# Gated linear recurrence in a hybrid decoder layer: key factor moved into the exponent as a logarithm, four-deep buffer ring

## What is computed

```python
q = silu(q); f = lb + (1 - lb) * sigmoid(f_logit)
k = 1 - f
b = cumsum(log(f))                       # inside a chunk of tokens
att[t, s] = sum_c q[t,c] * exp(b[t,c] - b[s,c]) * k[s,c]   (s <= t)
out   = att @ v + (q * exp(b)) @ state
state = exp(b_last) * state + (k * exp(b_last - b)).T @ v
```

## Time and profile before

| | |
|---|---|
| median of three runs | 2096.21 us |
| profiled execution | 2096.91 us |
| its span on the core | 2095.2 us |
| TensorE, VectorE, ScalarE, GpSimd busy | 94%, 76%, 63%, 30% of the span |
| granted TensorE clock, mean | 0.974 |
| recurrence | from about 352 us to about 473 us |

### The profile page before, as it was taken

One profiled execution on the slowest core, in us unless ns is written; L12 is line 12 of the kernel. 1 busy time (PEld: TensorE's weight loads), 2 busy tenths in 40 slices (PEclk: granted clock), 3 DMA queues, 4 the chain that ended last, 5 costly groups with the idle time before them and its releaser, 6 DMA issues. The chain is left out here.

```text
span 2095.2 us, 39510 instructions
## 1 busy us (share of the span) xinstructions
PE 1969.3 (94%) x11146; PEld 1685.9 (80%) x11147; DVE 1590.9 (76%) x2207; ACT 1323.3 (63%) x1914; POOL 638.5 (30%) x753
## 2 busy tenths in 40 slices
PE   7999988878977899999999999999999999999993
PEld 6887867767765878889798897979898888978882
DVE  5333156985668788889888898889888898988985
ACT  5221156563345676877768677687778677776875
POOL 2200011220234232524325243344334252332522
PEclk9999989999987999999999999999999999999997
DMA  5222120004346989989899898999899898999988
GB/s 190 69 81 61 50 102 2 14 18 137 121 146 228 318 288 311 336 277 365 280 321 320 286 368 272 336 318 370 281 346 304 295 350 271 357 293 306 338 278 308
DMA packets 266493, 508.75 MB, mean 243 GB/s; under 512 B 39266, under 2 KB 40290, under 8 KB 266180
## 3 DMA queue, kind: packets, MB, share of 16 engines
q1 hardware_dynamic: 243000, 457.91, 63.4%
q0 software_dynamic: 23440, 50.15, 9.1%
HBM read 466.50 MB, written 41.47 MB: 242 GB/s over the span
## 5 line engine op out<-in xcount | busy, mean ns | idle before, releaser
L2065 DVE TENSOR_TENSOR wlo<-raw,whi 128x1024 fp32r<-128x1024 f32 x770 | 921.7, 1219 | 79.3 <-ACT whi L1478 69.4
L1478 ACT ACTIVATE whi<-raw 128x1024 fp32r<-128x1024 f32 x771 | 844.3, 1115 | 152.8 <-PE ps L1128 109.6
L1126 PE MATMUL ps<-xT,whi 128*128 128x320 f32 x1920 | 504.8, 349 | 6.3 <-issue 5.7
L1128 PE MATMUL ps<-xT,wlo 128*128 128x160 f32 x1920 | 456.1, 238 | 0.0
L1126 PEld LDWEIGHTS ps<-xT,whi 128*128 128x128 f32 x1920 | 363.3, 189 | 9.9 <-issue 6.1
L1128 PEld LDWEIGHTS ps<-xT,wlo 128*128 128x128 f32 x1920 | 369.3, 192 | 0.5
L2348 POOL DMA_INDIRECT acc_d<-y,icur x96 | 175.4, 1827 | 438.3 <-ACT y L1516 256.9
L670 PE MATMUL ps<-whi,xT 128*128 128x512 f32 x544 | 218.7, 402 | 1.5 <-DVE xT L2088 1.5
L672 PE MATMUL ps<-whi,xT 128*128 128x512 f32 x544 | 213.7, 393 | 0.0
L671 PE MATMUL ps<-wlo,xT 128*128 128x512 f32 x544 | 213.2, 392 | 0.0
L670 PE MATMUL ps<-whi,aT 128*128 128x512 f32 x512 | 212.5, 415 | 0.0
(11 more groups left out here) (327 smaller groups left out, 3466.4 us busy)
## 6 DMA issues: line engine op xcount, KB each, us to landing
raw<-in_w SPq DMA_DIRECT2D x780, 512.0 KB
raw<-in_w_in SPq DMA_DIRECT2D x16, 512.0 KB
xs<-in_x SPq DMA_DIRECT2D x8, 512.0 KB, 10.5
raw<-in_w_out SPq DMA_DIRECT2D x8, 512.0 KB
mix<-in_x SPq DMA_DIRECT2D x8, 512.0 KB, 3.7
h_d<-h SPq DMA_DIRECT2D x8, 512.0 KB
acc_d<-mix SPq DMA_DIRECT2D x8, 512.0 KB
mix<-acc_d SPq DMA_DIRECT2D x8, 512.0 KB, 6.5
```

What stands on the lines that cost most here:

```text
L1126: pe.matmul(o2, wh[:, a, cols], xT2[:, :, k, 0:JOB_T], start=q == 0 and a == 0, stop=False, skip_group_check=True)
L1128: m = pe.matmul(o, wl[:, a, cols], xT2[:, 0, k, 0:JOB_T], start=False, stop=q == QUARTERS - 1 and a == 1, skip_group_check=True)
L1478: act.activation(parted(slot(whis, s)), paired(raw_slot(s), s), ACT.Copy).then_inc(split_hi, 1)
L2065: dve.tensor_tensor(parted(slot(wlos, s)), paired(raw_slot(s), s), parted(slot(whis, s).bitcast(F32)), ALU.subtract).then_inc(split_lo, 1)
```

## The change

The key product is replaced by a sum inside the exponent: k * exp(b_mid - b) = exp(b_mid - (b - ln k)). A new array, called shift, holds b - ln(k + 1e-35) and takes the place of the keys in `mix`.

- ScalarE takes the logarithm of the keys in four instructions of 128x1024 behind unit 1, after the write of the keys to `keys_d` has landed. VectorE makes the shift in four instructions behind unit 2. GpSimd's queue writes it to `shift_d`, and ScalarE's copies to `hv` in unit 4 wait for that write. `mix` is loaded from `shift_d`.
- The four `prods` instructions of step 7 and the 28 of the early halves (line 1787) are gone. The query product is made in place in `he`; `hp` is gone. TensorE's levels and transposes read `he`.
- `he` is one ring of four buffers. Arguments of step s wait until TensorE has used step s - 4 (or, where that is the last step of a head, until its products are made).
- GpSimd's early halves read the shift in `mix` in place of b.
- The diagonal still needs the keys: SyncE loads them from `keys_d`, one head at a time, into `hkey` (512 KB each).

```diff
-    he = at("he", B + 48 * KB, [P, 2, T])
-    hp = at("hp", B + 56 * KB, [P, 2, T])
+    he = at("he", B + 48 * KB, [P, RING, T])
...
+        def ring_free(engine, s):
+
+            if s < RING:
+                return
+            if (s - RING) % STEPS > LEVELS:
+                engine.wait_ge(prod_dve, prods_by(s - RING))
+            else:
+                engine.wait_ge(level_used, used_by(s - RING))
...
+            sp.wait_ge(keys_out, 16)
+            sp.dma_start(hkey[:, :, :], keys_d[:, :, 0:P]).then_inc(hkey_in, 16)
...
+                if hd + 1 < HH:
+                    sp.wait_ge(diag_done, hd + 1)
+                    sp.dma_start(hkey[:, :, :], keys_d[:, :, (hd + 1) * P:(hd + 2) * P]).then_inc(hkey_in, 16)
...
-                    v = hp[:, s % 2, t * P:(t + 1) * P]
+                    v = he[:, s % RING, t * P:(t + 1) * P]
...
-                        act.wait_ge(keys_out, 16)
+                        act.wait_ge(shift_out, 16)
...
+                    act.wait_ge(keys_out, 16)
+                    for hd in range(HH):
+                        k = keys[:, :, hd * P:(hd + 1) * P]
+                        act.activation(k, k, ACT.Ln, bias=tiny[:, 0:1]).then_inc(logs_set, 1)
...
-                        m = act.activation(he[:, s % 2, t * P:(t + 1) * P], hf[:, hd, t * P:(t + 1) * P], ACT.Exp,
+                        m = act.activation(he[:, s % RING, t * P:(t + 1) * P], shift_cols(hd)[:, t, :], ACT.Exp,
...
+                    dve.wait_ge(sums_set, HH)
+                    for hd in range(HH):
+                        dve.wait_ge(logs_set, HH + hd + 1)
+                        k = keys[:, :, hd * P:(hd + 1) * P]
+                        dve.tensor_tensor(k, by_tile(hf[:, hd, :]), k, ALU.subtract).then_inc(sums_set, 1)
...
-                    ov, kv, ev = (z.rearrange("p t (m two h) -> p t m two h", two=2, h=h)[:, :, :, 0, :]
-                                  for z in (by_tile(hp[:, s % 2, :]), key_cols(hd), by_tile(he[:, s % 2, :])))
-                    dve.tensor_tensor(ov, kv, ev, ALU.mult).then_inc(prod_dve, 1)
-                elif L == LEVELS:
-                    dve.tensor_tensor(by_tile(hp[:, s % 2, :]), key_cols(hd), by_tile(he[:, s % 2, :]),
-                                      ALU.mult).then_inc(prod_dve, 1)
...
+            pool.wait_ge(sums_set, 2 * HH)
+            pool.dma_start(shift_d, keys[:, :, :]).then_inc(shift_out, 16)
...
+                    ring_free(pool, s)
+                    bv, ev = (z.rearrange("p (t n) -> p t n", n=P).rearrange("p t (m two h) -> p t m two h", two=2, h=h)
+                              for z in (hf[:, hd, :], he[:, s % RING, :]))
+                    cv = shift_cols(hd).rearrange("p t (m two h) -> p t m two h", two=2, h=h)
+                    pool.tensor_tensor(ev[:, :, :, 0, :], bv[:, :, :, 0, h - 1:h].broadcast_to([P, NT, 64 // h, h]),
+                                       cv[:, :, :, 0, :], ALU.subtract).then_inc(arg_low, 1)
```

## The result

The changed kernel takes 2082.72 us (median of four runs, 2081.89 to 2085.01) against 2095.22 beside it: ratio 0.9942, 95% interval 0.993 to 0.9954. Run again later among the experiments it gave 0.9953 (0.9942 to 0.9965). Predicted were 2082.0 and a gain of 14.2 us; the two comparisons put the gain at 12.2 and 9.8 us (0.0058 and 0.0047 of 2095).

A forecast was written before the change was run, and what follows sets the result against it. The prediction took GpSimd and three VectorE instructions in one line to bound the recurrence. Gains of 2.7 + 3.5 + 6.0 + 2.0 = 14.2 us took 2096.9 to 2082.7, or 2082.0 for the median; range 2075 to 2091.

The forecast's parts named there:

- One head in the steady state: Recurrence, from one head's level 6 exponential to the next: 24.9 us instead of 27.94, 3.0 less; two such heads 6.0.
- GpSimd's new operand: GpSimd's early halves reading the shift in `mix`: cost taken as 0, upper end 0.5 us more per instruction.
- Middle of a head: Middle levels of a head: 2.26 us a level instead of 2.87, with GpSimd's instruction beside the mask copy.
- Start: First exponentials to level 6 of head 0: six levels save 3.7 us, less one GpSimd instruction of 1.04; 2.7 left.
- Head 0 to head 1: First head's turn, where ScalarE has no squares and no split: 3.5 us less by the steady head's addition.
- Tail: Last head's level 6 exponential to the next stage: 2.0 us less, from the key product's 1.2 and a clock share of 0.8.
- the clock's half share of 1.7: Last outputs, slowed by TensorE's reduced clock: none or all of 1.7 us might come back; half, 0.8, was taken.
- The cover of the front and of the queues: Ahead of the recurrence: logarithms, shift and extra DMA cost 0; uncovered, up to 9.7 us on ScalarE and 4.9 on VectorE.
- 1.04 still its plain duration: Sign of being right: GpSimd's early-half instruction in the recurrence still takes 1.04 us when nothing holds it.
- VectorE as the only bound: Rival, recurrence: VectorE bounds throughout, so all 22.0 us of removed products show; 2073 to 2078 us, chance 0.12.
- The chain keeping most of the gain: Rival, head's turn: collisions, ScalarE and TensorE's order leave only the middle levels' gain, 7.3 us, or 2089; chance 0.22.
- GpSimd beside nothing: Rival, levels: GpSimd runs after the copy, not beside it; 3.12 us a level, 7.0 us slower, 2103; chance 0.06.

The follow-up runs named there:

- experiment 4: Changed kernel with halves swapped: VectorE makes the early halves with the operand in `mix`, GpSimd the late halves with the plain operand; ratio 0.9943.
- experiment 7: The changed kernel itself, unedited, run and profiled a second time; 2083.64 us, ratio 0.9953 against the kernel before.
- experiment 5: Changed kernel with GpSimd held until the product right before a PSUM read of VectorE; 2080.5 us, ratio 0.9945 against the kernel before.
- experiment 6: Changed kernel with both edits: halves swapped between VectorE and GpSimd, and GpSimd held until VectorE's PSUM reads; 2078.43 us, ratio 0.9933 against the kernel before.

## Why the prediction came out right, and which terms did not

**The total.** 2082.0 against 2082.72, with the right sign and mechanism; 2.0 of its 14.2 us are not there by the first comparison, 4.4 not by the second, and 4.2 not in the stretch. The profiled pair differs by 11.9 only because 1.7 us lie ahead of the stretch, 1.0 of them ahead of the change too. And the prediction starts from 2096.21, where the kernel before took 2095.22 beside the changed one, which hides another 1.0. That the total came within 0.7 is luck in part: by the stretch, 4.2 of the 14.2 did not come.

**One head in the steady state**, point by point from the exponential of level 6 (392.57):

| point | predicted | measured |
|---|---|---|
| eight pieces end | 5.35 | 5.35 |
| states start (their copy) | 11.35 | 11.15 |
| outputs start | 14.0 | 13.93 |
| levels start again | 17.4 | 17.35 |
| next exponential of level 6 | 24.9 | 25.46 |

The chain held to 0.2 us up to the levels, the two collisions at the turn included. (The 13.1 that the prediction gives for the states before is the row behind their copy; the copy itself started 12.8 in, at 410.73.) The step that failed is "GpSimd's new operand: I take 0". It was 0.46 at level 5 and 0.59 at level 6 of the heads, inside the bound of 0.5 or near it, and with it came the held product of level 3; experiment 4 without it gives 24.87. VectorE's row of the same pattern was the wrong neighbour: its 695 ns with `mix` against 693 without, in experiment 4 and the changed kernel, say nothing about GpSimd.

**Middle of a head.** 2.26 was predicted for a level. Mask copies of head 1 start at 388.47, 391.00 and 393.22: 2.53 and 2.22. The 2.53 is the level where GpSimd's long level 6 reaches past the copy.

**Start**, 2.7 predicted, 1.4 measured: mis-sized. I let one of GpSimd's instructions land in front of a product. VectorE's rows in that part are 1.31, 1.63, 1.29, 1.99 and 1.12, five of them. And 0.6 went with the fall of the clock at 356 to 360, by the start of 13.65 in experiment 7; the prediction had no term for it. **Head 0 to head 1**, "the same addition gives 3.5", measured 2.3: from the states on it is the steady head (14.3 us from 378.27 to 392.57, and 14.31 from 403.72 to 418.03), where the operand's 0.6 is missing again, and GpSimd's two instructions in a row (372.02, 2.13) hold the late half at 373.43 for 0.6 that the sum left out.

**Tail**, 2.0 predicted, 1.3 measured: the product's 1.2 came; the clock's half share of 1.7 did not, the fall simply moved along with the idle time.

**The cover of the front and of the queues** held in every piece; ahead of `ak` 1.70 us were to spare, where the prediction had 1.4.

**The signs named.** Of the signs of being right, the distance of the middle levels, the length of a head, GpSimd's release by a level and TensorE's place in units 3 and 4 came. "1.04 still its plain duration" did not, and two signs of being wrong came too: GpSimd's 1.50 and 1.63, and VectorE's late halves of 1.1 to 1.7.

**The rivals.** VectorE as the only bound: no, 22.4 us busy in 25.46, stalls included. The chain keeping most of the gain (7.3): the stretch's 10.0 lies between it and the forecast. GpSimd beside nothing: wrong in sign, but its mechanism is what took the missing part; with GpSimd's reads away the stretch is 7.1 shorter. That whoever issues first makes the other stand still is what the turn shows at 399.16 and 401.50 and what experiments 5 and 6 turn round. The argument against this rival, that what releases GpSimd also releases the copy, is so in the middle of a head. At the turn the transposes and the step 8 product release it and there is no copy, and the prediction counted two instructions of 1.04 there, rightly. What it missed is that this price could be avoided: it took the earliest start that the buffers allow for the best one.

## What to carry to other kernels

Work that stretches another engine's when the two meet is priced by where it lands, and not only by how long it is: a wait moved back so that GpSimd starts right before VectorE's PSUM reads gained 3 us over three heads, where releasing it as early as the buffers allow lost them. Four buffers gained nothing while the key products stayed, and 10 us of stretch went with both changes together. A wait must be judged by what is queued behind it and by what it releases at once: two buffers cost 59 us here. Compare parts of a stage, and look at the granted clock in each, before a difference of 1 us is given a cause. Price a changed operand pattern on the engine that gets it, or give it to the engine whose rows show that it is free.

## What was not expected of the hardware

- GpSimd's subtraction of 128x512 took 1.04 us at every level in the kernel before, where nothing held it. With the operand in `mix`, whose pattern adds a step over the tiles, it took 1.50 at level 5 (runs of 2 elements) and 1.63 at level 6 (runs of 1); in experiment 5 both took 1.51 or 1.52. VectorE took 0.69 either way. No run separates the added step from the place of the array.
- Beside VectorE's PSUM copies and states GpSimd's instruction is a little longer than 1.04 with either operand (1.06 to 1.27). No run here tells why.
- TensorE's clock went to half in the last outputs after 2.83 us of idle time, in both kernels, and stayed full there once the gap was filled; the next fall then followed the next gap. Other falls move between executions of one kernel: the changed kernel had one at 356 to 360 us (0.60) and none in its heads, and in its second profile none there and one at 424 to 432 (0.77 and 0.80). So a saving of a few us that opens new idle time on TensorE can be lost again in the total.
